# Two-layer encoder trunk with 16 routed experts: experts behind the first two taken by falling number of token blocks

## What is computed

```python
def hier_moe(x, w_rg, b_rg, w_re, b_re, w_gate, w_up, w_down):
    g_prob = softmax(xt @ w_rg + b_rg)                 # 4 groups
    g_val, g_idx = top_k(g_prob, 1)
    e_logits = (xt @ w_re + b_re).reshape(-1, 4, 4)    # 4 experts in each group
    e_val, e_loc = top_k(e_logits of group g_idx, 2)
    combine = softmax(e_val) * g_val, put at the two chosen experts
    for e in range(16):
        h = silu(xt @ w_gate[e]) * (xt @ w_up[e])      # 2048 -> 512
        out = out + combine[:, e:e + 1] * (h @ w_down[e])   # 512 -> 2048
```

```
layer 0: 32 25 19 30 20 23 25 38 38 38 41 39 36 25 36 47   blocks 1 1 1 1 1 1 1 2 2 2 2 2 2 1 2 2  (24)
layer 1: 29 30 23 38 28 32 24 30 26 35 34 27 36 33 46 41   blocks 1 1 1 2 1 1 1 1 1 2 2 1 2 2 2 2  (23)
```

## Time and profile before

| | |
|---|---|
| median of three executions | 1815.03 us |
| profiled execution | 1809.38 us |
| its span, first to last instruction | 1807.7 us |
| mean granted TensorE clock | 0.941 |
| TensorE matmuls busy | 1585.4 us (88%) |
| VectorE busy | 927.3 us (51%) |
| ScalarE busy | 527.1 us (29%) |
| moved by DMA | 547.21 MB, mean 303 GB/s |

### The profile page before, as it was taken

The page is one execution under the profiler, slowest core; times in us unless marked ns, Lnnn a source line. Parts: engine busy times, 40 slices in busy tenths (PEclk is TensorE's granted clock), DMA queues, the critical chain, the costliest instruction groups (busy, mean ns, idle before and its releaser), DMA issues.

```text
span 1807.7 us, 34515 instructions
## 1 busy us (share of the span) xinstructions
PE 1585.4 (88%) x14628; PEld 1055.9 (58%) x14629; DVE 927.3 (51%) x1440; ACT 527.1 (29%) x612; POOL 47.4 (3%) x32
## 2 busy tenths in 40 slices
PE   6999999996775699998899999999697876797994
PEld 5999899873222244443399989998542322243442
DVE  7657556546322245554666574565462422344556
ACT  5552444323101021111455543543310101111112
POOL 0004000000000000000000040000000000000000
PEclk9999999998888899999999999999898988899997
DMA  8553455596999999999655444556979999999982
GB/s 304 181 175 129 140 176 178 197 371 283 422 422 422 422 422 422 421 417 421 246 180 184 158 138 147 176 186 231 404 303 421 422 422 421 422 422 422 422 363 93
DMA packets 139056, 547.21 MB, mean 303 GB/s; under 512 B 23044, under 2 KB 26344, under 8 KB 88296
## 3 DMA queue, kind: packets, MB, share of 16 engines
q1 hardware_dynamic: 138596, 546.13, 77.4%
q10 hardware_dynamic: 388, 0.04, 0.0%
HBM read 544.04 MB, written 2.10 MB: 302 GB/s over the span
## 4 chain that ended last, share of the span: by engine, by line
PE 68%; SPq 18%; DMA 8%; DVE 3%; issue 1%; DVEq 1%; ACT 0%; ACTq 0%
PE ps L735 23%; PE ps L960 11%; SPq L395 11%; PE ps L874 10%; SPq L399 7%; DMA room<-in_w_down_dram 6%; PE ps L978 6%; PE ps L732 5%; PE ps L943 4%; PE ps L924 3%; DMA room<-in_w_up_dram 1%; PE ps L932 1%; DVE h L1017 1%; DVE room L1020 1%; PE ps L811 0%
## 5 line engine op out<-in xcount | busy, mean ns | idle before, releaser
L960 PE MATMUL ps<-room 128*32 128x256 f32 x6016 | 388.7, 417 | 125.7 <-DMA room<-in_w_up_dram 121.9
L1017 DVE TENSOR_TENSOR w_lo<-room,w_hi 128x2048 fp32r<-128x2048 f32 x120 | 281.0, 2351 | 239.0 <-ACT w_hi L468 238.5
L960 PEld LDWEIGHTS ps<-room 128*32 128x32 f32 x6016 | 205.2, 118 | 322.2 <-DMA room<-in_w_up_dram 160.4
L735 PE MATMUL ps<-hT_hi,w_hi 128*128 128x256 f32 x1152 | 331.7, 288 | 6.2 <-DVE hT_lo L1017 6.2
L735 PE MATMUL ps<-hT_hi,w_lo 128*128 128x256 f32 x1152 | 328.6, 285 | 0.0
L735 PE MATMUL ps<-hT_lo,w_hi 128*128 128x256 f32 x1152 | 328.6, 285 | 0.0
L1017 DVE TENSOR_TENSOR h<-h,ps 128x512 f32<-128x512 f32 x392 | 242.8, 681 | 103.1 <-PE ps L943 102.9
L468 ACT ACTIVATE w_hi<-room 128x2048 fp32r<-128x2048 f32 x120 | 228.5, 1915 | 227.6 <-PE ps L735 111.0
L1017 DVE TENSOR_TENSOR room<-room,ps 128x128 f32<-128x128 f32 (+2 forms) x53 | 18.5, 353 | 412.6 <-ACT room L664 409.4
L735 PEld LDWEIGHTS ps<-hT_hi,w_hi 128*128 128x128 f32 x1152 | 223.8, 194 | 9.2 <-DVE hT_lo L1017 6.6
L735 PEld LDWEIGHTS ps<-hT_hi,w_lo 128*128 128x128 f32 x1152 | 223.7, 194 | 0.7 <-issue 0.5
(11 more groups left out here) (226 smaller groups left out, 1373.5 us busy)
## 6 DMA issues: line engine op xcount, KB each, us to landing
room<-in_w_gate_dram SPq DMA_DIRECT2D x128, 1024.0 KB, 23.3
room<-in_w_up_dram SPq DMA_DIRECT2D x128, 1024.0 KB, 25.6
room<-in_w_down_dram SPq DMA_DIRECT2D x128, 1024.0 KB, 20.5
room<-in_w_in_dram SPq DMA_DIRECT2D x88, 1024.0 KB, 5.0
room<-in_w_out_dram SPq DMA_DIRECT2D x32, 1024.0 KB, 5.0
room<-in_ln_g_dram SPq DMA_DIRECT2D x5, 1024.0 KB, 7.0
room<-in_ln_b_dram SPq DMA_DIRECT2D x5, 1024.0 KB, 8.2
h<-in_x_dram SPq DMA_DIRECT2D x4, 512.0 KB, 6.1
```

The source lines that it names most:

```text
L735: last = eng.matmul(ps[:, b + o // 2, (o % 2) * T:(o % 2) * T + T], w_[:, o * P:o * P + P], x_[:, kk, :], start=opens and o % 2 == 0, stop ...
L960: last = eng.matmul(ps[r0:r0 + BLK, 0, 0:2 * P], xe[:, x0:x0 + BLK], unit_gu(u)[:, :, k, c * P:c * P + P], start=(i == 0 and k == 0), stop ...
L1017: return eng.tensor_tensor(o, a, b, op)
```

## The change

The table is now ordered. VectorE gives each expert a key, 16 times its further blocks plus 15 less its number; experts 0 and 1 (`FIXED`) get 2000 and 1000 more instead, so that they stay first. Comparing all keys with all keys (16 x 16) says which experts stand ahead of an expert: the sum of their blocks is its first block, and their number is its place. A second comparison, of places with 0 to 15, brings rows 0 and 1 into the order of places and gives the expert's number at each place (row 2 now; the total is in row 4). With the counts above, layer 0 is taken as 0, 1, then 7 8 9 10 11 12 14 15 with two blocks each, then 2 3 4 5 6 13; layer 1 as 0, 1, then 3 9 10 12 13 14 15, then 2 4 5 6 7 8 11.

SyncE reads the number of the expert at a place from the table and adds it to the address of that expert's DMAs. The first block's gather, copy and turn have signals of their own (`first_hot`, `first_gathered`, `first_rows`, `first_turned`) that are waited for with constants, so they no longer need the registers with the first block's number; those are read just ahead of the loops.

```diff
+    FIXED = 2
...
+                def weights(w, e):
+                    if e < FIXED:
+                        return w[l, e]
+                    return w.rearrange("l e a b -> (l e) a b")[bass.ds(l * E + number, 1)].rearrange("o a b -> (o a) b")
...
                 for u in range(PER_E * E):
                     e, i = u // PER_E, u % PER_E
+                    if e >= FIXED and i == 0:
+                        number = expert_row(eng, 2, e)
...
-                            src = w[l, e].rearrange("(p k) n -> p k n", k=KD)
+                            src = weights(w, e).rearrange("(p k) n -> p k n", k=KD)
...
+            eng.iota(first_key[:], pattern=[[-1, 16]], base=15, channel_multiplier=0, ...)
...
+            for e in range(FIXED):
+                eng.memset(first_key[:, e:e + 1], 1000.0 * (FIXED - e))
...
-                eng.wait_ge(tab_ready.sem, tab_ready.at(l, 1))
-                g0, nb = expert_row(eng, 1, 0), expert_row(eng, 2, 0)
                 eng.wait_ge(hk_ready.sem, hk_ready.at(l, NT))
-                gather(g0 + 2 * l + 1)
-                turn_rows(g0 + l + 1)
+                gather(first_hot.sem, first_hot.at(l, 1), first_gathered.sem)
+                turn_rows(first_rows.sem, first_rows.at(l, 1), first_turned.sem)
                 eng.wait_ge(wts_ready.sem, wts_ready.at(l, 1))
...
                 last.then_inc(spread_done.sem, 1)
+                eng.wait_ge(tab_ready.sem, tab_ready.at(l, 1))
+                g0, nb = expert_row(eng, 1, 0), expert_row(eng, 4, 0)
...
-                eng.tensor_tensor_scan(scn[:, 0, :], tab[:, 0, :], ones[:, 0:16], 0.0, ALU.add, ALU.add)
-                eng.drain()
-                eng.scalar_tensor_tensor(tab[:, 1, :], scn[:, 0, :], 1.0, tab[:, 0, :], ALU.subtract, ALU.subtract)
+                eng.scalar_tensor_tensor(key, tab[:, 0, :], 16.0, first_key[:], ALU.mult, ALU.add)
                 ts(tab[:, 0, :], tab[:, 0, :], 1.0, None, ALU.add)
+                eng.drain()
+                tt(sorted_by, key ... [P, 16, 16], key ... [P, 16, 16], ALU.is_gt)
+                eng.drain()
+                tt(table_by[:, 0], sorted_by, tab[:, 0:1, :].to_broadcast([P, 16, 16]), ALU.mult)
+                eng.drain()
+                eng.tensor_reduce(tab[:, 1, :], table_by[:, 0], AX.X, ALU.add)
...
-                mark()
+                mark(first_hot.sem)
+                eng.tensor_reduce(expert_at, sorted_by, AX.X, ALU.add)
                 ts(tab[:, 1, :], tab[:, 1, :], carry[:], None, ALU.add)
...
+                tt(sorted_by, expert_at ... [P, 16, 16], iota[:, 0:16] ... [P, 16, 16], ALU.is_equal)
+                eng.drain()
+                for r0, r1 in ((0, 2), (2, 3)):
+                    n = r1 - r0
+                    tt(table_by[:, 0:n], tab[:, r0:r1] ... [P, n, 16, 16], sorted_by ... [P, n, 16, 16], ALU.mult)
+                    eng.drain()
+                    eng.tensor_reduce(tabf[:, r0:r1], table_by[:, 0:n], AX.X, ALU.add)
+                    eng.drain()
+                eng.tensor_copy(tabi[:, 0:3, :], tabf)
...
-                g0, nb = expert_row(eng, 1, 0), expert_row(eng, 2, 0)
-                take_rows(g0 + l + 1)
+                take_rows(first_turned.sem, first_turned.at(l, 1))
```

More of the change, by code:

```diff
@@ L192, in trunk @@
         tab = small(426, (3, 16))
-        scn = small(474, (1, 16))
+        total = small(474, (1, 1))
+        key, expert_at, tabf = small(0, (1, 16))[:, 0, :], small(16, (1, 16))[:, 0, :], small(80, (3, 16))
+        sorted_by = lgp.rearrange("p (e n) -> p e n", e=16)
+        table_by = xe.rearrange("p (r e n) -> p r e n", r=2, e=16)
         t32 = sb("t32", [P, 2, NT, 16])
@@ L916, in _, with gather @@
                 eng.matmul(ps[:, 1, 32:48], ones[:], M[:, 2, 1, :], start=False, stop=True).then_inc(ranks_done.sem, 1)
-                def gather(count):
-                    eng.wait_ge(hot_ready, count)
+                def gather(ready, count, done):
+                    eng.wait_ge(ready, count)
                     for t in range(NT):
@@ L926, in gather, with turn_rows @@
                                               start=(t == 0), stop=(t == NT - 1), tile_position=(0, r0))
-                    last.then_inc(xrow_done, 1)
-                def turn_rows(count):
-                    eng.wait_ge(xrow_ready, count)
+                    last.then_inc(done, 1)
+                def turn_rows(ready, count, done):
+                    eng.wait_ge(ready, count)
                     for q in range(4):
                         last = eng.transpose(ps[:, 3, q * P:q * P + P], xrow[:, q * P:q * P + P], ident[:])
-                    last.then_inc(xT_done, 1)
+                    last.then_inc(done, 1)
                 def scatter(g, t):
@@ L965, in expert_block @@
                     last.then_inc(gu_done, 1)
-                    gather(g + 2 * l + 2)
+                    gather(hot_ready, g + l + 1, xrow_done)
                     scatter(g, 0)
@@ L1379, in _, with mark @@
                 eng.drain()
-                def mark():
+                def mark(ready):
                     tt(hot_2[:], block_iota.rearrange("p (o u s) -> p o u s", o=1, u=1).to_broadcast([P, 2, NT, BLK]),
@@ L1408, in _, with take_rows @@
                 tt(wts[:, 1], wts[:, 0], ex[:, :, 4:5], ALU.mult).then_inc(wts_ready.sem, 1)
-                def take_rows(count):
+                def take_rows(done, count):
                     g_, b_ = (lnc[:, 2 * l + 1, i, :].rearrange("p (c q o) -> p q c o", q=4, o=1).to_broadcast([P, 4, 4, BLK])
@@ L1414, in take_rows @@
                     x4 = xe.rearrange("p (q c s) -> p q c s", q=4, c=4)
-                    eng.wait_ge(xT_done, count)
+                    eng.wait_ge(done, count)
                     tt(x4, ps[:, 3, :].rearrange("p (q c s) -> p q c s", q=4, c=4), g_, ALU.mult)
```

51 lines of the change are left out of this document (32 added, 19 removed).

## The result

Median of four executions 1782.09 us (1779.97 to 1783.13), against 1814.97 us for the kernel before (four, 1811.89 to 1817.3): ratio 0.9818, 95% interval 0.9801 to 0.9836. I had stated 1788.6 us, with 1784 to 1797 as the range. The direction is right, and the gain is about 33 us where I had worked out 26.4.

A forecast was written before the change was run, and what follows sets the result against it. Expert stages were taken as bound by loading their weights. Tails of 34.5 us less 4.1 (ring), 2.8 (start), 0.6 (into layer 1) and 0.6 (last block) gave 26.4 us: 1815.03 - 26.4 = 1788.6 us, range 1784 to 1797.

The forecast's parts named there:

- the start's 2.8 us: Start of each expert stage: VectorE's longer table makes the first block 1.4 us later, 2.8 us lost in both layers.
- The tails, 34.5 us: End of both expert stages, TensorE work after loading stops: falling order takes away at most 16.2 and 18.3 us.
- the last block: Last one-block expert of each layer: its end doesn't always sit on the DMA's; 0.3 us a layer lost, 0.6 together.
- The ring, 4.1 us: Runs of two-block experts: SyncE gets weight slots back later and DMA dips; 2.3 us more in layer 0, 1.8 in layer 1.
- SyncE, 0: Address arithmetic on 168 DMAs a layer: hidden behind the DMA's 2.48 us each, so taken as 0.
- Into layer 1, 0.6: After layer 0's last down product: next weights queue behind the last expert's, second quarter rounded 0.6 us later.
- The end: End of layer 1: last block starts once its weights are complete; no term in the sum for what follows.
- The cold first block: Rival, chance 0.17: first block's products start at the slow clock, 3.4 us a layer lost; 1795.4 us.
- The dry ring: Rival, chance 0.08: each of 15 two-block experts loses 1.17 us for want of free slots; 1801.5 us.
- SyncE starved: Rival, chance 0.03: SyncE's issue takes longer than 2.48 us and starves 336 DMAs; 1861 us at 2.7 us an issue.
- the order that doesn't come about: Rival, chance 0.02: experts come in the order as before, only the start's 2.8 us remain; 1817.8 us.

The follow-up runs named there:

- e7_warm: e4_gather_only plus eight 128x128 products of constants on TensorE between the counts and the gather; 1806.88 us, ratio 0.9957 to the kernel before.
- e3_by_number: The changed kernel with the key's factor 0 instead of 16, so experts are taken by number; 1814.31 us, ratio 1.0004 to the kernel before.
- e5_rising: The changed kernel with the key's factor -16 instead of 16, so two-block experts come last; 1823.15 us, ratio 1.0045 to the kernel before.
- e2_after: The changed kernel, unchanged, run again beside the others on one chip; 1781.79 us, ratio 0.9822 to the kernel before.
- e13_after_c: The changed kernel, unchanged, one more execution for its trace; 1779.6 us.
- e12_two_light: The changed kernel with hand-written constant keys: two two-block experts, one one-block expert in turn, one-block experts last; 1778.59 us, ratio 0.9815 to before.
- e4_gather_only: The kernel before with only the first block's own signals and later register loads, its table and order kept; 1810.24 us, ratio 0.9979.
- e9_before_warm: The kernel before with only eight 128x128 products of constants between the counts and the first gather; 1810.06 us, ratio 0.9987.

## Why the prediction was wrong

The step that failed is this one: "the median of the timed runs is 5.65 us above that execution, so I state 1815.03 - 26.4 = 1788.6 us". I took the 5.65 us for an offset that both kernels have. Against the execution that I read it from, the sum gives 1783.0, and the profiled execution of the changed kernel took 1782.46. That these agree so well is in part luck: in that trace the stage of layer 0 lasts 444.3 us, against 446.6 and 445.8 in the other two of the changed kernel, and layer 1 up to its router 1.5 us more than in them. Part of the 5.65 us was a cost of before that the change takes away, and the term that was mis-sized by it is the start's 2.8 us: measured as a mean it is 0.1.

In six traces of before there are twelve starts of a stage: six take 12.20 to 12.81 us from the last count to the first products, and six 14.53 to 14.87. Their mean is 13.60. The execution on which the sum stood had two fast ones, 2.2 us less together than two of the mean length; the other 3.4 of the 5.65 us lie elsewhere. In three traces of the changed kernel the six starts take 13.65 to 13.69 whatever the spread does, since VectorE's queue of 2.29 us product and row work ends last, or as late as the slow spread. So in the typical case the later first block costs nothing: 0.1 us for both layers instead of 2.8. That it is the clock that parts fast from slow is shown by the granted clock of the two executions above, and by e7_warm.

The Trainium skill, "TensorE: Matmul & The Clock Gate", section "What's actually happening", says that one and the same kernel runs another number of products at the slow rate in each run, and puts the whole effect under 1% of a typical span. The traces agree: a start differs by 2.3 us, and executions of before by some 8 us or 0.4% in all, of which the starts are one part. For a change of this size that is as much as the terms of the sum.

By parts, as means over six traced executions of before and three of the changed kernel (lengths in us, from the trace's rows; a router's part begins with the turn of `h` behind the output projection, a stage runs from its first gate and up product to the end of its last down product):

| part | before | after | gain | forecast |
|---|---|---|---|---|
| up to layer 0's router | 400.3 | 400.5 | -0.2 | 0 |
| both routers, tables, first blocks' rows | 64.7 | 63.9 | 0.8 | -2.8 |
| experts of layer 0 | 459.1 | 445.6 | 13.5 | 13.6 |
| experts of layer 1 | 460.2 | 443.1 | 17.1 | 16.2 |
| into layer 1 | 14.5 | 14.9 | -0.4 | -0.6 |
| layer 1 up to its router | 383.1 | 383.1 | 0.0 | 0 |
| after the last down product | 29.4 | 28.5 | 1.0 | 0 |
| span | 1811.4 | 1779.5 | 31.9 | 26.4 |

Put right by the start alone, the sum would state 1785.9 us, and 3.8 would still be missing. The table has 0.9 of them in layer 1's stage, 1.0 at the end and 0.9 in the routers; the last differ by as much from one execution of the same kernel to the next.

Point by point:
- *The tails, 34.5 us: right.* Together with the dips and the last block I forecast 13.6 and 16.2 for the two stages. e3_by_number, which leaves out the order alone, has none of it, and e5_rising loses instead. Read directly, from the last weights' transfer to the end of the last down product, the tails were 19.9 and 21.8 us as means of the six traces of before and are 4.5 and 4.3 now: 33.0 us less, where 34.5 - 0.6 is 33.9.
- *The ring, 4.1 us: right in kind, nearly in place.* Slices of 1 us under 365 GB/s lose 2.2, 3.9 and 3.7 us in layer 0 of the three traces, where I had 2.9; and 1.0, 0.9 and 1.2 in layer 1, where I had 1.8. In e2_after and e13_after_c layer 0 has a fourth dip one expert earlier (at 618 and 616 us), where I had the fifth two-block expert with some reserve. The smaller loss in layer 1 is probably most of what that layer gained above the forecast. e12_two_light takes the dips away, and its stages are 2.7 and 0.1 us shorter: the dips cost what they last in layer 0, and hardly anything in layer 1.
- *The start: every time of it right, the comparison wrong*, as above. The starts lose 0.1 us in that row of the table; that the row gains 0.8 lies in the routers ahead of the counts, where both kernels run the same code.
- *SyncE, 0: right as far as it shows.* e3_by_number keeps its 336 addressed DMAs and costs nothing, and the first release goes out 3.72 us behind the first products in both kernels (436.24 - 432.52 and 434.89 - 431.17).
- *Into layer 1, 0.6: measured 0.4.* This is little against what it varies by: one trace of each kernel has 15.2 us there, the others 14.3 and 14.8. The second rounding waits for its weights, 0.70 us, in ScalarE's rows:

```profile
877.59 1.91 ACT L488 ACTIVATE w_hi<-room 128x2048 fp32r<-128x2048 f32 x1
880.20 1.91 ACT L488 ACTIVATE w_hi<-room 128x2048 fp32r<-128x2048 f32 x1 [0.70 <-DMA room<-in_w_in_dram]
```

- *The end: missed, 1.0 us.* In two of the three executions the last down product of layer 1 itself waits for its weights (1.50 us in e13_after_c), so the scatter of the block before is already past and what follows is 1.5 us shorter. I had the last block starting when its weights are there and did not follow what waits behind it.

*The rivals.* The cold first block didn't come: its first 84 records take 4.74 us in the rows above, 56 ns each, and 128 take 7.11 at full rate. A slow clock does cost, but ahead of the first block, and before rather than after. The dry ring would have given 1801.5, and stretches of 160 us at 422 GB/s exclude it. SyncE starved is excluded by the same stretches, and the order that doesn't come about by the ends of the stages.

*The range.* Its low end took in better terms of the sum only, and not that the profiled execution of before might be one that drew both starts fast; 5.65 us between that execution and the median were a sign of it. The means explain 31.8 us; the medians differ by 32.5 to 32.9. The rest is within the intervals, and not resolved. Nor are these: why the dips of layer 0 vary between executions, what decides the level of the clock at a start, and the 0.9 us by which the medians of e3_by_number and e4_gather_only differ beyond their starts. In the one trace of each, the stages of e3_by_number are 1.0 and 1.6 us longer, and in layer 1 that is the slow piece and gather shown above; whether this holds for other executions, and whether SyncE's addresses have a share in layer 0, was not tested.

## What to carry to other kernels

Where a stage is bound by loads and its work comes in uneven parts, keep the light parts for the end, more than one of them, and spread the others among the heavy ones ahead of it, so that the ring never runs dry. Before a sum is made against one profiled execution, ask why it lies apart from the median: if some segment has two lengths, price the change against both. A short chain of products behind an idle TensorE can be shortened by products of constants ahead of it, when the engine would be idle there anyway (1.1 and 2.1 us a start here); where another wait lies between the two, part of it can be lost again, as in layer 0 of e9_before_warm.

## What the runs showed of the hardware that was not expected

- The same instructions in the same place had the clock at 0.50 or at 1.00 from one execution of before to the next; gather, turn and spread took 3.25 to 3.64, 0.66 and 1.95 us, or 3.64, 1.12 and 3.35 to 3.62. A start was 2.3 us longer by it.
- Eight products of 128x128 ahead of the gather made it 2.35 us long instead of 3.64 and the spread 1.95 instead of 3.31; the ratio to before went from 0.9979 to 0.9957 (two chips), 4 us over two layers, of which the earlier first products are 3.2 (1.1 in layer 0, 2.1 in layer 1).
- A reduction takes as long as a product of its input: 0.42 us for 256 elements, 0.69 for 512.
- Adding a number read from the table to the addresses of 336 DMAs cost nothing that shows: ratio 1.0004 (0.9996 to 1.0013) with it and the rest of the change but the order.
